# A decoder step's gated MLP on one core: block products by Strassen's scheme, and the down projection apart

## What is computed

```python
def conv_ffn(h, conv_state, w_up, w_conv, b_conv, w_down):
    S = h.shape[1]
    u = h @ w_up
    gate = u[..., :D_FF]
    up = u[..., D_FF:]
    ext = jnp.concatenate([conv_state.astype(gate.dtype), gate], axis=1)
    conv = ext[:, 0:S] * w_conv[0] + b_conv
    for tap in range(1, CONV_WIDTH):
        conv = conv + ext[:, tap:tap + S] * w_conv[tap]
    act = jax.nn.silu(conv.astype(F32)) * up.astype(F32)
    return act.astype(h.dtype) @ w_down, ext[:, S:]
```

## Time and profile before

| | |
|---|---|
| median of 3 runs | 3012.2 us (3009.78 to 3012.58) |
| profiled execution, its own time | 3013.36 us |
| span of the profiled execution | 3011.4 us |
| mean granted TensorE clock | 0.983 |
| TensorE busy | 2887.3 us, 96% |
| VectorE busy | 1557.7 us, 52% |
| ScalarE busy | 753.0 us, 25% |
| POOL busy | 302.4 us, 10% |
| first MLP, up matmuls (L906) | 749 to 1485 us |
| second MLP, up matmuls (L906) | 2231 to 2967 us |

### The profile page before, as it was taken

The page is one execution under the profiler, slowest core; times in us unless marked ns, Lnnn a source line. Parts: engine busy times, 40 slices in busy tenths (PEclk is TensorE's granted clock), DMA queues, the critical chain, the costliest instruction groups (busy, mean ns, idle before and its releaser), DMA issues. The chain is left out here.

```text
span 3011.4 us, 51059 instructions
## 1 busy us (share of the span) xinstructions
PE 2887.3 (96%) x21226; PEld 2661.4 (88%) x21226; DVE 1557.7 (52%) x2993; ACT 753.0 (25%) x1305; POOL 302.4 (10%) x262
## 2 busy tenths in 40 slices
PE   8999999889999999999989999988899999999998
PEld 7888899779999999999987666655899999999998
DVE  3444444453655555555553444487356555555554
ACT  4444311343211111111242333322231111111113
POOL 3101132002000000000131000042010000000001
PEclk9999999899999999999989999999899999999999
DMA  6121111672888521111112000176221111111101
GB/s 198 50 72 50 36 52 36 241 282 63 279 293 292 209 61 51 42 43 41 42 62 85 16 1 1 53 299 262 91 63 55 58 42 42 56 42 42 42 28 68
DMA packets 204272, 288.88 MB, mean 96 GB/s; under 512 B 13114, under 2 KB 175956, under 8 KB 196500
## 3 DMA queue, kind: packets, MB, share of 16 engines
q1 hardware_dynamic: 195672, 177.78, 18.5%
q0 software_dynamic: 8448, 108.93, 9.8%
HBM read 263.95 MB, written 88.40 MB: 117 GB/s over the span
## 5 line engine op out<-in xcount | busy, mean ns | idle before, releaser
L906 PE MATMUL psum<-mlp_halves,w_up 128*128 128x352 f32 x6336 | 1012.3, 321 | 0.0
L906 PEld LDWEIGHTS psum<-mlp_halves,w_up 128*128 128x128 f32 x6336 | 1008.2, 188 | 0.8
L944 PE MATMUL psum<-acts,w_down 128*128 128x352 f32 x3168 | 516.1, 323 | 4.6 <-DVE xT L1115 3.2
L944 PEld LDWEIGHTS psum<-acts,w_down 128*128 128x128 f32 x3168 | 510.0, 188 | 6.1 <-DVE xT L1115 3.8
L1115 DVE TENSOR_TENSOR xT<-xT,psum 128x352 f32<-128x352 f32 x528 | 274.9, 521 | 240.9 <-PE psum L944 240.9
L1424 PE MATMUL psum<-h_ab,w_in_halves 128*128 128x352 f32 x2016 | 341.2, 326 | 3.4 <-PEq L280 2.3
L1424 PEld LDWEIGHTS psum<-h_ab,w_in_halves 128*128 128x128 f32 x2016 | 322.5, 189 | 17.2 <-issue 10.9
L988 ACT CAST acts<-window 128x1056 fp32r<-128x1056 f32 x44 | 47.4, 1077 | 705.8 <-PE psum L944 570.8
L606 PE MATMUL psum<-mlp_halves,project_w 128*128 128x352 f32 x1152 | 188.8, 326 | 8.4 <-DVE project_w L634 8.4
L606 PEld LDWEIGHTS psum<-mlp_halves,project_w 128*128 128x128 f32 x1152 | 187.5, 192 | 9.0 <-DVE project_w L634 8.6
L983 ACT ACTIVATE conv<-conv 128x1072 f32<-128x1072 f32 x44 | 48.4, 1100 | 534.9 <-DVE conv L1089 534.9
(11 more groups left out here) (335 smaller groups left out, 3438.6 us busy)
## 6 DMA issues: line engine op xcount, KB each, us to landing
mlp_raw<-in_w_up SPq DMA_DIRECT2D x88, 512.0 KB, 5.1
out_new_a_k_s<-in_cache_a_k POOLq DMA_DIRECT2D x8, 4088.0 KB, 15.5
out_new_a_v_s<-in_cache_a_v POOLq DMA_DIRECT2D x8, 4088.0 KB, 14.8
mlp_raw<-in_w_down SPq DMA_DIRECT2D x22, 1024.0 KB, 6.5
w_in_raw<-in_w_in_ab SPq DMA_DIRECT2D x28, 512.0 KB, 4.5
xT<-x_spill SPq DMA_DIRECT2D x2, 4224.0 KB, 15.4
ws_k_rows<-in_cache_a_k SPq DMA_DIRECT2D x8, 1024.0 KB, 9.4
ws_v_rows<-in_cache_a_v SPq DMA_DIRECT2D x8, 1024.0 KB, 9.6
```

What stands on the lines that cost most here:

```text
L906: mm = nc.tensor.matmul(c.bank[TILES * part + n][:, 0:TILE], w_up[s][:, w, part, k, :], h[:, x, k, tokens_of(n)], start=k + w + x == 0, st ...
L944: mm = nc.tensor.matmul(c.bank[6 + t % 2][:, 0:TILE], w_down[:, w, s, o * P:(o + 1) * P], acts[s][:, x, tokens_of(n)], start=s + w + x == ...
```

## The change

In each chunk after the first, token tiles 1 and 2 and the two halves of the 1024 input features are taken as 2 x 2 blocks, gate and up weights as the other 2 x 2 blocks, and their product is made from 7 block products instead of 8, by Strassen's scheme in the form with shared sums. The third token tile is multiplied as before. One block product is 4 slices x 3 = 12 matmuls. A chunk ("round") is 11 steps of 12: P1, P6, gate of tile 3 (first half), P3, P2, gate of tile 3 (second half), P5, P7, up of tile 3 (two steps), P4.

- **Token side** ("turns"): three sums of token blocks, `TURN_1` to `TURN_3`, are formed once per layer by POOL (1408 columns each, 4 + 3 instructions), `TURN_4` by VectorE. They are rounded and rested like any operand.
- **Weight side:** each chunk has 8 operands of 512 columns: the four whole blocks and four sums. POOL forms the sums with 5 instructions (`form`). ScalarE rounds each of the 8, VectorE makes each rest. The split operands have one buffer, refilled one operand at a time as soon as its last use in the running chunk is over; the raw weights have one buffer too.
- **Result side:** VectorE combines the products with 7 additions. All 8 PSUM banks are in use.
- **Activations** are stored to HBM (`products_spill`) instead of being split and used at once.
- **Down projection:** a phase behind the loop, written out: 3 token tiles x 2 halves of the outputs, 6 passes of 22 slots. A slot of the ring (8 buffers) holds 128 x 512 down weights and 128 x 352 products, loaded by two DMAs, split by ScalarE and VectorE, and used by 12 matmuls. Sums stay in 4 PSUM banks over the 22 slots of a pass; `xT` is added to once per output tile.
- **Rolled cache:** in layer 0 POOL issues one of the 16 copies in each half of groups 1 to 8, and waits for it before it forms `SUM_3`.
- The final stage's row transposes move to fixed slots of the down phase.

The loads and the weight operands:

```diff
+    def load_up(self, sp, g, s):
+
+        for part in range(2):
+            sp.dma_start(self.raw[:, part], self.up_rows[:, :, bass.ds(g * 2 * P + (s * P + part * D_FF), P)]).then_inc(self.up_loaded, 16)
...
+    def form(self, pool, g, s, waits):
...
+        pool.wait_ge(self.up_loaded, START + (self.chunk(g, s) + 1) * 32)
+        waits(self.SUM_2)
+        tt(into(self.SUM_2), whole(self.UP_1), whole(self.UP_2), ALU.add).then_inc(self.formed, 1)
+        pool.wait_ge(self.formed, done + 1)
+        tt(into(self.SUM_2), into(self.SUM_2), whole(self.GATE_1), ALU.subtract).then_inc(self.formed, 1)
+        waits(self.SUM_4)
+        pool.wait_ge(self.formed, done + 2)
+        tt(into(self.SUM_4), whole(self.GATE_2), into(self.SUM_2), ALU.subtract).then_inc(self.formed, 1)
+        waits(self.SUM_1)
+        tt(into(self.SUM_1), whole(self.UP_1), whole(self.UP_2), ALU.add).then_inc(self.formed, 1)
+        waits(self.SUM_3)
+        tt(into(self.SUM_3), whole(self.GATE_1), whole(self.UP_1), ALU.subtract).then_inc(self.formed, 1)
...
+                def load_next(g, s):
+                    sp.wait_ge(self.w_split, START + (self.round_of(g, s) + 1) * 8)
+                    sp.wait_ge(self.formed, START + (self.round_of(g, s) + 1) * 5)
+                    if s == 0:
                         self.load_up(sp, g, 1)
-                        self.load_down(sp, g)
...
+                    else:
+                        self.load_up(sp, g + 1, 0)
```

TensorE's steps of a chunk (the waits that the prediction speaks of; `second` is only the first chunk of this kind):

```diff
+                    products(self.BANK_3, self.SUM_4, tokens(1, 1), True, True)
+                    split_of(self.GATE_2)
+                    combined(1, 7)
+                    if second:
+                        multiplied()
+                    products(self.BANK_2, self.GATE_2, tokens(1, 0), True, True)
```

`combined(1, 7)` is the seventh addition of the chunk before, the one that takes P4 out of its bank. VectorE's work of a chunk; `refill` makes the rests of the next chunk's operands:

```diff
+                    self.wait_step(dve, g, s, self.P6)
...
+                    plus(third_sum, first_product, product_of(self.BANK_6), 1)
+                    refill(self.GATE_1)
+                    self.wait_step(dve, g, s, self.P2)
+                    plus(first_gate, first_product, product_of(self.BANK_2), 2)
+                    refill(self.SUM_2)
...
+                    tt(first_gate, first_gate, norm.scale[:, 0, :], ALU.mult).then_inc(self.gate_taken, 1)
+                    refill(self.SUM_4)
...
+                    take_last_gate(s, bank[self.BANK_LAST_GATE])
+                    refill(self.GATE_2)
...
+                    plus(fourth_sum, third_sum, product_of(self.BANK_5), 3)
+                    plus(second_gate, fourth_sum, product_of(self.BANK_3), 4)
...
+                    convolve(g, s, False)
+                    refill(self.SUM_1, self.SUM_3, self.UP_1)
...
+                    scale_conv(g, s)
+                    self.wait_step(dve, g, s, self.P4)
+                    plus(third_sum, third_sum, product_of(self.BANK_4), 7)
+                    refill(self.UP_2)
+                    dve.wait_ge(self.combined, done + 7)
+                    multiply(g, s, (third_sum, fourth_sum, bank[self.BANK_LAST_UP]), lambda n: None)
```

More of the change, by code:

```diff
@@ L699, in turn @@
         pe.wait_ge(added[0], added[1] + KC * ((b * P + rows_of(b) - 1) // TILE + 1))
[L700 to L703 removed]
+        if b == 4:
+            pe.wait_ge(self.moved, START + 3)
         for k in range(KC):
@@ L756 @@
 class Mlp:
+    GATE_1, GATE_2, UP_1, UP_2, SUM_2, SUM_4, SUM_1, SUM_3 = range(8)
+    TURN_2, TURN_1, TURN_4, TURN_3 = range(4)
+    ORDER = (GATE_1, SUM_2, SUM_4, GATE_2, SUM_1, SUM_3, UP_1, UP_2)
+    ORDER_FIRST = (SUM_2, SUM_4, SUM_1, SUM_3, GATE_1, GATE_2, UP_1, UP_2)
+    STEPS = 11
+    P1, P6, GATE_LAST_1, P3, P2, GATE_LAST_2, P5, P7, UP_LAST_2, UP_LAST_1, P4 = range(1, STEPS + 1)
+    LAST_USE = {GATE_1: GATE_LAST_1, SUM_2: P6, SUM_4: P3, GATE_2: GATE_LAST_2, SUM_1: P5, SUM_3: P7, UP_1: UP_LAST_1, UP_2: P4}
+    HALF = KC // 2
+    BANK_1, BANK_6, BANK_3, BANK_5, BANK_2, BANK_7, BANK_LAST_GATE, BANK_LAST_UP = range(8)
+    BANK_4 = BANK_2
+    SUMS = 7
+    WIDE = D_MODEL // 2
+    RING_AT = (101376, 0, 134144, 117760, 6912, 13824, 142336, 125952)
+    RING = len(RING_AT)
+    PASSES = 2 * TILES
+    OUTS = D_MODEL // 2 // P
+    LAST_K = FC - 1
     def __init__(self, c):
@@ L848, in __call__ @@
         tails = c.at(f"tails{call}", [P, FC, TAIL], F32, 167808)
-        temps = [c.at(f"norm_temps{x}_{call}", [P, norm.TEMPS], F32, (150528, 117760)[x]) for x in range(2)]
-        rows = raw[0:TAIL].rearrange("p a n -> p (a n)")[:, 0:D_FF]
+        temps = [c.at(f"norm_temps{x}_{call}", [P, norm.TEMPS], F32, (150528, 33792)[x]) for x in range(2)]
+        rows = c.at(f"tail_rows{call}", [TAIL, D_FF], F32, 22528)
         sums = norm.sum_up(temps[0][:])
```

915 lines of the change are left out of this document (597 added, 318 removed).

## The result

The changed kernel takes 3221.7 us (median of four executions, 3221.0 to 3228.2) beside 3011.0 for the kernel before on the same chip (3009.4 to 3012.6): a ratio of 1.070, with a 95% interval from 1.069 to 1.072. It is 210.7 us slower; the forecast was 183 slower (3195).

A forecast was written before the change was run, and what follows sets the result against it. TensorE bounds the kernel before; after the change the loop of waits through the single raw buffer sets the chunk period. Layer 1 +89 and layer 0 +94 us make +183: 3195 us, own range 3155 to 3240, stated range 3055 to 3245.

The forecast's parts named there:

- The matmuls saved: Chunks after the first take 132 matmuls for 144: 504 fewer over two layers, 80.4 us of TensorE.
- The way around: Chunk loop through the single raw buffer: rest and issue 0.9, loads 5.7, POOL 6.8, VectorE 12.8, period 26.2 us.
- VectorE's sum of 17.5: VectorE's own work per chunk adds up to about 17.5 us, fitting TensorE's 21.1 by sum but not by order.
- SUM_2's rest comes behind all of them: In the chunk loop POOL starts all five sum instructions when the load lands; VectorE's rest of SUM_2 follows all five.
- rival 2: POOL does not hold VectorE's rests: period 23.6 us in layer 1, 26 beside copies, whole 3073 us; chance 0.14.
- The copies: Layer 0's rolled-cache copies overlap some 3 us of the next load: period 26.9 us in 16 chunks, otherwise 26.2.
- The start: From an MLP's first up matmul to chunk 1's sum with P4: 81.6 us, with POOL's turned tokens delaying VectorE.
- Nothing to wait for: Chunk 1 of an MLP, started at 60 us, reaches its sum with P4 21.6 us later without waiting.
- The down phase: Starts 14.5 us behind the last-but-one chunk's sum with P4; TensorE binds: 252.8 us matmuls, 2.6 transposes, 3 added.
- Rival 3: In the down phase the ring's loads at 200 GB/s starve TensorE: +35 us a layer, whole 3265 us; chance 0.08.
- Rival 4: TensorE's 5 us pauses per chunk lower its clock, but the slower matmuls fit the 5.1 us slack; no chance given.
- Rival 1: TensorE binds all along: 80.4 us saved less some 10 at the two starts, whole 2942 us; chance 0.10.

The follow-up runs named there:

- e1: Changed kernel with a second buffer for the raw up weights (the convolution's two buffers become one): 2994.0 us, 0.9936 of the kernel before.
- e2: Changed kernel, one raw buffer, POOL's five sums per chunk cut to 8 columns, whole blocks rounded and rested in their place: 3001.1 us.
- e3: Changed kernel with POOL's sums cut to 8 columns, plus five 512-column POOL additions per chunk that nobody reads or waits for: 3195.7 us.
- e8: Changed kernel, one raw buffer, its 16 copies of 4 MB in layer 0 cut to 4 rows each: 3204.6 us.
- e5: Changed kernel plus second raw buffer, with POOL's seven 1408-column instructions for the turned tokens cut to 4 columns: 2962.5 us.
- e4: Changed kernel with 24 thrown-away matmuls more in each chunk but an MLP's first, before the wait for P4's bank: 3213.9 us.
- e9: Changed kernel plus second raw buffer, two plain first chunks, first two turned tokens formed during the output projection, VectorE's work reordered: 2959.0 us, 0.9825 of before.

## Why the prediction was right, point by point

The sign, the mechanism and the size held; 28 us of the 211 were missing, and two parts were right in sum but not in their terms, which is partly luck. Layer 1 was forecast at 856 and took 863.7; layer 0 at 864 and took 882.1. In both the forecast's start was 5 us too long, which hides part of what the other terms lacked.

- **The matmuls saved, 80.4 us.** Right: 504 fewer, and 21.0 us a chunk as soon as nothing else binds (e1).
- **The way around, 26.2 us.** Measured 26.6 in layer 1. By the rows above: rest and issue 0.96 (forecast 0.9), load to POOL's start 5.84 (5.7), from there to the next rest of UP_2 19.67 (6.8 + 12.8 = 19.6). 19 periods make 505 us for 498. With the wait for the load taken out the period is TensorE's own 21.0 (e1), with POOL's sums taken out it is close to it, 21.6 (e2).
- **VectorE's sum of 17.5.** The terms listed add up to 16.9 with 0.60 a rest, and e2 shows 16.1 of it busy where POOL does not hold it up. Nothing in the forecast hangs on it: it only had to be under 21.1.
- **"SUM_2's rest comes behind all of them".** This picture was wrong in detail: the rest starts behind POOL's third instruction, ends behind the fourth, and then the fifth waits for it (1.73). The two take turns. From POOL's start to SUM_2's rest it is 4.4 us, not 6.8, and from there to UP_2's rest 15.3, not 12.8; the two errors cancel, since POOL's last two instructions are paid for behind the rest's start instead of ahead of it.
- **POOL holds VectorE up (rival 2 out).** Right. With the sums taken out the rests are at 692 ns, and 5.0 us a chunk go; with work for nobody added 3.2 of them come back (layer 1 of e3).
- **The copies, 0.7 us a chunk.** Too small: the mean period of layer 0 is 27.4 where the forecast's 16 chunks of 26.9 and 3 of 26.2 have a mean of 26.8, 12 us over 19 chunks, the largest miss. Some 7 of them are the way around itself, as in layer 1. The rest is the copies: e8 gives 17 us for all, 1.1 for each, and shows the overlap of copy and load costing the load 1.2 us (6.3 for 5.1) where I had put 0.7.
- **The start, 81.6 us.** Measured 77.0 and 76.4, but by other terms. VectorE left the norm at 20 (forecast 22). The first block product came at 45, not 60, and its chunk took 31.6 us, not 21.6. "Nothing to wait for" was wrong: the way around holds in this chunk already. In layer 1 UP_2's rest ends 7 us behind the first block product, POOL starts on the next load 5.7 us later, and the sum with P4 comes 18.8 us behind that. That the two errors cancel to 5 us is luck. And the 6 us pause inside the first chunk was not foreseen: I followed the norm's rests but not the addition that stands behind them. e5 shows POOL's turned tokens as 16 to 18 us of it.
- **The down phase.** It started 15.0 us (17.7 in layer 0) behind the sum named, forecast 14.5. It took 267.2 and 266.0 us, forecast 262.4 and 258.4. By the windows above TensorE was idle 4.2 and 5.4 us where the forecast had 3, most of it in the first 50 us; 1.5 and 3.0 of it are waits for ScalarE to take the transposed tails out of their bank. The other 3.6 and 5.2 us are busy time that the forecast left out, in layer 0 in part the next norm's 8 matmuls (3 us). Rival 3 (the ring starves TensorE) is out: 222 GB/s were delivered and TensorE was busy 98%.
- **Rival 4 (the clock).** It came true and cost nothing, as forecast: the granted clock was 0.93 in layer 1's loop (it fell to 1.2 GHz for a few us behind many of the pauses), and e4, at 0.99, has the same period there (26.7 for 26.6).
- **Rival 1 (TensorE binds).** It needed the way around under 21.1 us. That is what the second buffer does, and then the kernel is faster than before, though by 19 us and not by the 70 that this rival counted: of the 40 us of matmuls saved in each layer 26 and 34 are lost again, 16 and 17 of them by POOL's turned tokens at the start (e5, by the MLPs' times). With the start mended (e9) an MLP takes 739 us for 770 and 767.

## What to carry to other kernels

When matmuls are saved, add up not only each engine's busy time but the way around every single-buffered tile: rest, issue, load, sums, rest. Here VectorE had 16.1 us of its own work in a chunk (e2) for TensorE's 21.1, and the loop still took 26.5, because one 8 KB buffer per partition tied the engines in a row; the buffer was worth 228 us. And work given to POOL is not free beside a VectorE that reads SBUF: count it as VectorE's time wherever someone waits for VectorE, keep its instructions short there, or place it where VectorE is idle.
